# Seven block products instead of eight for one expert pair in four, in the value stage of a PEER layer

## The chip, the cores and the metric

The kernel runs on one core of one Trainium2 chip. The metric is the device time of one execution, in microseconds (us). The kernel before took 2188.84 us (median of three runs: 2188.84, 2189.22 and 2179.97). Engines are named as in the profile: PE multiplies matrices and PEld loads its stationary operand, DVE is the vector engine, ACT the scalar engine, POOL is GpSimd, SP issues the transfers.

## The reference

Two layers, 256 tokens, 1024 channels. Each layer is a mixer (retention, RWKV-7, gated linear attention), an output projection, and a product-key retrieval over 16384 single-neuron experts:

```python
act = gelu(einsum('td,ted->te', xb, u[eidx])) * gate     # 16 experts of each of 8 heads per token
x = x + einsum('te,ted->td', act, v[eidx])
```

The kernel computes it densely. It makes a full matrix of activations, experts by tokens, that is zero where an expert isn't chosen, and multiplies it with all of `v`. This last product, 256 tokens x 16384 experts x 1024 channels, is the value stage.

## The kernel before

One program of 128 expert blocks of 128 experts. `ACTS[:, e, :]` holds the activations of expert block `e`, experts on the partitions and 256 tokens along the row. The values of an expert block are 128 x 1024 numbers, in two halves of 512 channels. Two expert blocks (1 MB) fill one half of `RING`, so `RING` holds one body of four expert blocks, that is eight halves `m = 0..7`.

Every product is in three parts for precision. A number is split into a high part, a cast to fp32r made by ACT (`EH` for the values, `AH` for the activations), and a low part, the rest, made by DVE as a subtraction (`EL`, `AL`). `v_half(m, j)` (L806 to L817) waits for the low parts and, for each of the two token tiles, issues high x high (L814), high x low (L815) and low x high (L816), 512 columns each, added in bank `2 * t + f` of PSUM. So a half is six matmuls, a body 48, and the 32 bodies of a layer 1536.

Nothing plans the order. Each engine has its own instruction queue, in program order, and counting semaphores tie them:

- ACT, `v_split` (L1048) and `a_split` (L1057): the high part of half `m` goes into slot `m % 4` of `EH` once the half four places before has left PE (`v_done`, one count per half). The activations have two slots.
- DVE, `v_lows` (L1688) and `a_lows` (L1692): the low part, once ACT's high part is there (`v_hi`, `a_hi`).
- SP (L366 to L368): reloads a half of the ring once its four low parts are made (`v_lo`).
- After the last body DVE adds the four banks to the residual `X` (L1852), the norm of the next layer begins, and SP clears the semaphores of the layer and releases the next one (`go`).

The first body is written out with the end of the stage before (the `u` stage, which computes the activations), the other 31 are a hardware loop on each engine.

Of the kernel before, what the change touches and what calls it, by code (L numbers as in the profile page):

```python
# [40 lines left out]
P = 128  # L41
# [24 lines left out]
GATE_SCALE = 2.0 ** 15  # L66
D_FEW, P_MANY = (2, 6), (0, 1, 3, 4, 5, 7)
# [35 lines left out]
def trunk(nc, x_in, w_in, w_out, cols, small, rows, norm_final, w_q, keys, u_t, v_t, const, xconst, out):  # L103
    with ExitStack() as ctx:
# [118 lines left out]
        DECODE = PS[:, 0:4, :].rearrange("p b n -> p (b n)").rearrange("p (m u n) -> p m u n", m=8, u=16)  # L223
        FROW = BIG[:, 0:D]
# [54 lines left out]
        vring = [sem("v0_landed"), sem("v1_landed")]  # L279
# [31 lines left out]


# [6 lines left out]
        def _(sp):  # L319
# [10 lines left out]
            with sp.Fori(0, L) as l:  # L330
# [30 lines left out]
                for i in range(2):  # L361
                    sp.wait_ge(*u_lows_made(4 * i + 2, N_BODY - 1, False))
                    sp.wait_ge(*u_lows_made(4 * i + 3, N_BODY - 1, False))
                    sp.dma_start(RING[:, i, :], v_t[l, i]).then_inc(vring[i], 16)
                with sp.Fori(1, 32) as j:
                    for i in range(2):  # L366
                        sp.wait_ge(v_lo, 8 * j + 4 * i - 4)
                        sp.dma_start(RING[:, i, :], v_t[l, 2 * j + i]).then_inc(vring[i], 16)  # L368
                for i in range(2):
                    sp.wait_ge(v_lo, 252 + 4 * i)  # L370
# [15 lines left out]
        def _(pe):  # L386
# [419 lines left out]
            def v_half(m, j, first):  # L806
                e, f = m // 2, m % 2
                pe.wait_ge(v_lo, 8 * j + m + 1)
# [8 lines left out]
                mm.then_inc(v_done, 1)  # L817

            with pe.Fori(0, L) as l:
# [71 lines left out]
                for m in range(8):  # L891
                    v_half(m, 0, True)
                with pe.Fori(1, 32) as j:
                    for m in range(8):
                        v_half(m, j, False)
                pe.wait_ge(v_done, 256)
# [5 lines left out]
        def _(act):  # L902
# [145 lines left out]
            def v_split(m, j, first):  # L1048
                if m % 4 == 0:
                    act.wait_ge(vring[m // 4], 16 * (j + 1))  # L1050
                if first and m < 4:
                    act.wait_ge(u_done, 253 + m)
                else:
                    act.wait_ge(v_done, 8 * j + m - 3)
                act.copy(EH[:, m % 4, :], RING[:, m // 4, (m % 4) * 512:(m % 4 + 1) * 512]).then_inc(v_hi, 1)  # L1055

            def a_split(e, j, first):  # L1057
                if first and e < 2:
                    if e == 0:
                        act.wait_ge(quad_out, 3 + N_QUAD)  # L1060
                else:
                    if first and e == 2:
                        act.wait_ge(u_mul, 2 + 128 - LATE)
                    act.wait_ge(v_done, 8 * j + 2 * e - 2)
                act.copy(AH[:, e % 2, :], ACTS[:, 4 * j + e, :]).then_inc(a_hi, 1)  # L1065

# [5 lines left out]
            with act.Fori(0, L) as l:  # L1072
# [208 lines left out]
        def _(dve):  # L1281
# [480 lines left out]
            with dve.Fori(0, L) as l:  # L1762
# [288 lines left out]
```

## Time and profile before

| what | before |
|---|---|
| median of three runs | 2188.84 us |
| profiled execution, own time | 2180.91 us |
| its span | 2179.1 us |
| PE busy | 2089.8 us, 96% |
| DVE busy | 1441.2 us, 66% |
| ACT busy | 1314.5 us, 60% |
| granted TensorE clock, mean | 0.986 |

The page of the profile gives the busy time of each engine, the span in 40 slices, the chain of work that ended last and the costliest groups of instructions. Busy times of PE overlap, because matmuls are pipelined; the pace is read from the starts. An instruction of DVE or ACT also has a duration longer than the distance to the start of the next one. Shares are averages over stages with different limits: the value stage is the one with 192 GB/s, slices 14 to 20 of the first layer.

### The profile page before, as it was taken

How to read it: one execution, taken by the hardware profiler on the slowest of the kernel's cores; microseconds unless marked ns; L12 is line 12 of the kernel's file. 1: busy time of each engine (PE TensorE's matmuls, PEld its weight loads, DVE VectorE, ACT ScalarE, POOL GpSimd, SP SyncE). 2: the span in 40 equal slices, each digit the busy share in tenths (PEclk: the TensorE clock that was granted, in tenths of full speed). 3: DMA queues.
4: the chain of work that ended last, by engine and by line, in shares of the span. 5: the costliest groups of instructions: out<-in, count | busy, mean ns of one | idle time of the engine just before them, and what ended most of it. 6: DMA issues, size and time to landing. Idle time of an engine off the chain costs nothing.

```text
span 2179.1 us, 45295 instructions
## 1 busy us (share of the span) xinstructions
PE 2089.8 (96%) x14548; PEld 1896.7 (87%) x14548; DVE 1441.2 (66%) x3050; ACT 1314.5 (60%) x3093; POOL 388.9 (18%) x342
## 2 busy tenths in 40 slices
PE   7889899999999999999998998999999999999997
PEld 7889499999999988888788895999999998888886
DVE  5764349778887666666567633496778886666665
ACT  5530145699999655555565302556999995555554
POOL 0312007632222100000003120175322220000000
PEclk9999999999999999999999998999999999999999
DMA  5320244444444555555552102444444445555554
GB/s 210 116 78 1 97 155 165 165 171 157 156 168 157 176 192 192 192 192 192 192 189 97 59 1 98 173 174 166 162 155 170 156 155 191 194 193 192 192 192 184
DMA packets 47464, 338.82 MB, mean 155 GB/s; under 512 B 5649, under 2 KB 5777, under 8 KB 6929
## 3 DMA queue, kind: packets, MB, share of 16 engines
q1 hardware_dynamic: 47376, 337.73, 43.2%
q8 instruction: 46, 0.75, 0.1%
q14 instruction: 42, 0.34, 0.0%
HBM read 336.66 MB, written 1.05 MB: 155 GB/s over the span
## 4 chain that ended last, share of the span: by engine, by line
PE 85%; DVE 9%; ACT 2%; DMA 2%; issue 1%; DVEq 0%; SPq 0%; ACTq 0%; PEldq 0%
PE ps L815 11%; PE ps L814 11%; PE ps L816 11%; PE ps L784 10%; PE ps L786 9%; PE ps L785 9%; PE ps L687 3%; PE ps L407 2%; PE ps L408 2%; PE ps L409 2%; PE ps L550 2%; PE ps L564 1%; PE ps L794 1%; PE ps L795 1%; PE ps L423 1%; DVE expert_lo L1320 1%
## 5 line engine op out<-in xcount | busy, mean ns | idle before, releaser
L784 PE MATMUL ps<-h_t_hi,expert_hi 128*128 128x256 f32 x2048 | 591.3, 289 | 12.3 <-DVE expert_lo L1686 8.5
L785 PE MATMUL ps<-h_t_lo,expert_hi 128*128 128x256 f32 x2048 | 578.5, 282 | 0.0
L786 PE MATMUL ps<-h_t_hi,expert_lo 128*128 128x256 f32 x2048 | 578.2, 282 | 0.0
L1869 POOL TENSOR_TENSOR expert_lo<-w_ring,expert_hi 128x512 fp32r<-128x512 f32 x204 | 289.8, 1429 | 772.1 <-ACT expert_hi L975 770.4
L784 PEld LDWEIGHTS ps<-h_t_hi,expert_hi 128*128 128x128 f32 x2048 | 391.6, 191 | 15.6 <-ACT big L980 8.2
L814 PE MATMUL ps<-expert_hi,act_hi 128*128 128x512 f32 x1024 | 398.4, 389 | 0.0
L815 PE MATMUL ps<-expert_lo,act_hi 128*128 128x512 f32 x1024 | 398.4, 389 | 0.0
L816 PE MATMUL ps<-expert_hi,act_lo 128*128 128x512 f32 x1024 | 398.3, 389 | 0.0
L785 PEld LDWEIGHTS ps<-h_t_lo,expert_hi 128*128 128x128 f32 x2048 | 392.0, 191 | 0.0
L786 PEld LDWEIGHTS ps<-h_t_hi,expert_lo 128*128 128x128 f32 x2048 | 391.6, 191 | 0.0
L975 ACT CAST expert_hi<-w_ring 128x512 fp32r<-128x512 f32 x512 | 308.0, 614 | 98.3 <-PE ps L786 83.7
L1690 DVE TENSOR_TENSOR expert_lo<-w_ring,expert_hi 128x512 fp32r<-128x512 f32 x512 | 331.5, 688 | 6.6 <-ACT expert_hi L1055 6.0
L1065 ACT CAST act_hi<-big 128x256 fp32r (+1 forms) x256 | 104.0, 406 | 321.3 <-PE ps L816 321.3
L1055 ACT CAST expert_hi<-w_ring 128x512 fp32r<-128x512 f32 x512 | 291.8, 617 | 3.2 <-PE ps L786 3.2
L1686 DVE TENSOR_TENSOR expert_lo<-w_ring,expert_hi 128x512 fp32r<-128x512 f32 x308 | 217.6, 718 | 107.1 <-ACT expert_hi L975 104.1
L1694 DVE TENSOR_TENSOR act_lo<-big,act_hi 128x256 fp32r<-128x256 f32 x256 | 108.8, 425 | 256.0 <-ACT act_hi L1065 256.0
L814 PEld LDWEIGHTS ps<-expert_hi,act_hi 128*128 128x128 f32 x1024 | 192.2, 188 | 40.1
L816 PEld LDWEIGHTS ps<-expert_hi,act_lo 128*128 128x128 f32 x1024 | 192.2, 188 | 40.0
L815 PEld LDWEIGHTS ps<-expert_lo,act_hi 128*128 128x128 f32 x1024 | 192.2, 188 | 39.6
L937 ACT CAST expert_hi<-w_ring 128x512 fp32r<-128x512 f32 x168 | 99.8, 621 | 118.9 <-PE ps L425 54.5
L1320 DVE TENSOR_TENSOR expert_lo<-w_ring,expert_hi 128x512 fp32r<-128x512 f32 x168 | 119.4, 749 | 65.4 <-ACT expert_hi L937 63.1
L407 PE MATMUL ps<-h_t_hi,expert_hi 128*128 128x256 f32 x448 | 128.1, 286 | 2.5 <-DVE expert_lo L1320 1.3
(294 smaller groups left out, 3279.2 us busy)
## 6 DMA issues: line engine op xcount, KB each, us to landing
w_ring<-u_t SPq DMA_DIRECT2D x128, 1024.0 KB, 4.8
w_ring<-v_t SPq DMA_DIRECT2D x128, 1024.0 KB, 4.8
w_ring<-w_in SPq DMA_DIRECT2D x32, 1024.0 KB, 4.8
w_ring<-w_q SPq DMA_DIRECT2D x16, 1024.0 KB, 4.8
w_ring<-w_out SPq DMA_DIRECT2D x8, 1024.0 KB, 4.8
big<-xconst SPq DMA_DIRECT2D x2, 1666.0 KB, 9.5
w_ring<-keys SPq DMA_DIRECT2D x2, 1024.0 KB, 4.7
big<-rows SPq DMA_DIRECT2D x2, 576.0 KB, 11.2
```

What stands on the lines that cost most here:

```text
L407: pe.matmul(o, w_hi_m[:, c, :], HTH[:, d, :], start=d == 0, stop=False)
L784: pe.matmul(o, w_hi[:, c, :], HTH[:, d, :], start=d == 0, stop=False)
L785: pe.matmul(o, w_hi[:, c, :], HTL[:, d, :], start=False, stop=False)
L786: mm = pe.matmul(o, w_lo[:, c, :], HTH[:, d, :], start=False, stop=d == DC - 1)
L814: pe.matmul(o, a_hi_t, EH[:, m % 4, :], start=start, stop=False, skip_group_check=True)
L815: pe.matmul(o, a_hi_t, EL[:, m % 4, :], start=False, stop=False, skip_group_check=True)
L816: mm = pe.matmul(o, a_lo_t, EH[:, m % 4, :], start=False, stop=True, skip_group_check=True)
L975: act.copy(EH[:, m % 4, :], RING[:, m // 4, (m % 4) * 512:(m % 4 + 1) * 512]).then_inc(u_hi, 1)
L1055: act.copy(EH[:, m % 4, :], RING[:, m // 4, (m % 4) * 512:(m % 4 + 1) * 512]).then_inc(v_hi, 1)
L1686: dve.tensor_tensor(EL[:, m % 4, :], RING[:, m // 4, (m % 4) * 512:(m % 4 + 1) * 512], EH[:, m % 4, :].bitcast(F32), ALU.subtract).then_in ...
L1690: dve.tensor_tensor(EL[:, m % 4, :], RING[:, m // 4, (m % 4) * 512:(m % 4 + 1) * 512], EH[:, m % 4, :].bitcast(F32), ALU.subtract).then_in ...
L1869: pool.tensor_tensor(EL[:, m % 4, :], RING[:, m // 4, (m % 4) * 512:(m % 4 + 1) * 512], EH[:, m % 4, :].bitcast(F32), ALU.subtract).then_i ...
```

## The change

The 32 bodies of a layer become a first body, 15 turns of two bodies each, and a last body. A turn has eight expert blocks, four pairs. Its first pair is multiplied by the seven-product form of a 2 x 2 block product, where the classic form takes eight block products (two expert blocks by two token tiles by two channel halves). With A the activations (A11, A12: token tile 0, first and second expert block; A21, A22: token tile 1) and B the values (B11, B12: first expert block, two channel halves; B21, B22: second one):

- sums of activations, 128 columns each, in `ASUM`: s1 = A21 + A22, s2 = s1 - A11, s3 = A11 - A21, s4 = A12 - s2
- sums of values, 512 columns each: T1 = B12 - B11, T3 = B22 - B12, T2 = T3 + B11, T4 = B21 - T2
- products, three matmuls each: p1 = A11 B11, p2 = A12 B21, p3 = s4 B22, p4 = A22 T4, p5 = s1 T1, p6 = s2 T2, p7 = s3 T3

p2, p3 and p4 go into the banks of their outputs; p1, p7, p6 and p5 are added up over all turns in the four other banks (4, 7, 6, 5) and folded into `X` and into each other by DVE in and after the last body. The other three pairs are classic (`c`, `d`, `e`, four halves each, six matmuls a half). A turn is 19 units in the order of `V_ORDER`, with the seven products spread between the halves. `V_SLOT` gives each unit one of six slots, two of them new, in memory of the `u` stage. All sums and low parts are made by DVE. The transfers of the values are cut from 1 MB to 512 KB.

The diff, cut to what decides the order of work:

```diff
+V_ORDER = ("p1", "p2", "p3", "c0", "c1", "p7", "c2", "c3", "p6", "d0", "d1", "p5", "d2", "d3", "p4", "e0", "e1", "e2", "e3")
+V_SLOT = (0, 1, 2, 3, 4, 0, 5, 1, 2, 3, 0, 4, 5, 1, 2, 0, 3, 4, 5)
+V_LEN, V_TURNS = len(V_ORDER), N_BODY // 2
+V_ALL = 8 + V_LEN * (V_TURNS - 1) + 8
...
+        VH, VL = ([*(e[:, s, :] for s in range(4)), h[:, 1024:1536], h[:, 1536:2048]] for e, h in ((EH, hth_flat), (EL, htl_flat)))
+        A11H, A2H, ASH = hth_flat[:, 0:128], hth_flat[:, 128:384], hth_flat[:, 512:1024]
+        A11L, A2L, ASL = htl_flat[:, 0:128], htl_flat[:, 128:384], htl_flat[:, 512:1024]
+        T1, T2, T3, T4 = (ht_flat[:, 512 * i:512 * (i + 1)] for i in range(4))
+        ASUM = HOTX[:, 0:512]
+        B11, B12, B21, B22 = (RING[:, 0, 512 * i:512 * (i + 1)] for i in range(4))
...
+        def v_at(name, k):
+            return V_LEN * k - 10 + V_ORDER.index(name)
+        def v_slot(name):
+            return V_SLOT[V_ORDER.index(name)]
+        def slot_left(name, k, first):
+            o = V_ORDER.index(name)
+            s, same = V_SLOT[o], [i for i in range(V_LEN) if V_SLOT[i] == V_SLOT[o]]
+            if o > same[0]:
+                return v_at(V_ORDER[same[same.index(o) - 1]], k)
+            if first:
+                return 5 + s if s < 4 else 1
+            return v_at(V_ORDER[same[-1]], k - 1)
...
+                def load_v(c, j):
+                    half = slice(c % 2 * D, (c % 2 + 1) * D)
+                    sp.dma_start(RING[:, c // 2, half], v_t[l, 2 * j + c // 2, :, half]).then_inc(v_landed[c], 16)
...
-                    sp.dma_start(RING[:, i, :], v_t[l, i]).then_inc(vring[i], 16)
-                with sp.Fori(1, 32) as j:
-                    for i in range(2):
-                        sp.wait_ge(v_lo, 8 * j + 4 * i - 4)
-                        sp.dma_start(RING[:, i, :], v_t[l, 2 * j + i]).then_inc(vring[i], 16)
+                    for c in range(2):
+                        load_v(2 * i + c, 0)
+                for c in range(4):
+                    sp.wait_ge(v_lo, 2 * c + 2)
+                    load_v(c, 1)
+                with sp.Fori(1, V_TURNS) as k:
+                    sp.wait_ge(t_made, 4 * k - 1)
+                    load_v(0, 2 * k)
+                    sp.wait_ge(t_made, 4 * k)
+                    load_v(1, 2 * k)
+                    sp.wait_ge(v_lo, v_at("c1", k))
+                    load_v(2, 2 * k)
+                    sp.wait_ge(v_lo, v_at("c3", k))
+                    load_v(3, 2 * k)
+                    sp.wait_ge(v_lo, v_at("d1", k))
+                    load_v(0, 2 * k + 1)
+                    sp.wait_ge(v_lo, v_at("d3", k))
+                    load_v(1, 2 * k + 1)
+                    sp.wait_ge(v_lo, v_at("e1", k))
+                    load_v(2, 2 * k + 1)
+                    sp.wait_ge(v_lo, v_at("e3", k))
+                    load_v(3, 2 * k + 1)
...
+            def v_product(name, j, bank, a_hi_t, a_lo_t, start):
+                pe.wait_ge(v_lo, v_at(name, j))
+                o, s = PS[:, bank, :], v_slot(name)
+                pe.matmul(o, a_hi_t, VH[s], start=start, stop=False, skip_group_check=True)
+                pe.matmul(o, a_hi_t, VL[s], start=False, stop=False, skip_group_check=True)
+                pe.matmul(o, a_lo_t, VH[s], start=False, stop=True, skip_group_check=True).then_inc(v_done, 1)
+            def v_classic(name, j, e, f):
+                pe.wait_ge(v_lo, v_at(name, j))
+                s = v_slot(name)
+                for t in range(NT):
+                    o = PS[:, 2 * t + f, :]
+                    a_hi_t, a_lo_t = AH[:, e, t * P:(t + 1) * P], AL[:, e, t * P:(t + 1) * P]
+                    pe.matmul(o, a_hi_t, VH[s], start=False, stop=False, skip_group_check=True)
+                    pe.matmul(o, a_hi_t, VL[s], start=False, stop=False, skip_group_check=True)
+                    mm = pe.matmul(o, a_lo_t, VH[s], start=False, stop=True, skip_group_check=True)
+                mm.then_inc(v_done, 1)
...
+                pe.wait_ge(a_lo, 8 * k - 3)
+                v_product("p1", k, 4, A11H, A11L, first)
+                pe.wait_ge(a_lo, 8 * k - 2)
+                v_product("p2", k, 0, A2H[:, a12], A2L[:, a12], False)
+                pe.wait_ge(s_lo, k)
+                v_product("p3", k, 1, ASH[:, s4], ASL[:, s4], False)
+                pe.wait_ge(a_lo, 8 * k - 1)
+                v_classic("c0", k, 0, 0)
+                v_classic("c1", k, 0, 1)
+                v_product("p7", k, 7, ASH[:, s3], ASL[:, s3], first)
+                pe.wait_ge(a_lo, 8 * k)
+                v_classic("c2", k, 1, 0)
+                v_classic("c3", k, 1, 1)
+                v_product("p6", k, 6, ASH[:, s2], ASL[:, s2], first)
+                pe.wait_ge(a_lo, 8 * k + 1)
+                v_classic("d0", k, 0, 0)
+                v_classic("d1", k, 0, 1)
+                v_product("p5", k, 5, ASH[:, s1], ASL[:, s1], first)
+                pe.wait_ge(a_lo, 8 * k + 2)
+                v_classic("d2", k, 1, 0)
+                v_classic("d3", k, 1, 1)
+                v_product("p4", k, 2, A2H[:, a22], A2L[:, a22], False)
+                pe.wait_ge(a_lo, 8 * k + 3)
+                v_classic("e0", k, 0, 0)
+                v_classic("e1", k, 0, 1)
+                pe.wait_ge(a_lo, 8 * k + 4)
+                v_classic("e2", k, 1, 0)
+                v_classic("e3", k, 1, 1)
...
+            def b_high(name, src, j, first):
+                act.wait_ge(v_done, slot_left(name, j, first))
+                act.copy(VH[v_slot(name)], src).then_inc(v_hi, 1)
...
+                left("p1", 1)
+                act.copy(A11H, acts(0, 0, P)).then_inc(a_hi, 1)
+                landed(0, 2 * k - 1)
+                b_high("p1", B11, k, first)
+                landed(1, 2 * k - 1)
+                b_high("p2", B21, k, first)
+                left("p4", 1)
+                act.copy(A2H, acts(1, 0, S)).then_inc(a_hi, 1)
+                act.wait_ge(s_made, 3 * k)
+                left("p5", 1)
+                act.copy(ASH, ASUM).then_inc(s_hi, 1)
+                b_high("p3", B22, k, first)
+                left("e1", 6)
+                act.copy(AH[:, 0, :], acts(2, 0, S)).then_inc(a_hi, 1)
+                landed(2, 2 * k - 1)
+                b_high("c0", ring(4), k, first)
+                b_high("c1", ring(5), k, first)
+                act.wait_ge(t_made, 4 * k - 3)
+                b_high("p7", T3, k, first)
+                left("e3", 8)
+                act.copy(AH[:, 1, :], acts(3, 0, S)).then_inc(a_hi, 1)
+                landed(3, 2 * k - 1)
+                b_high("c2", ring(6), k, first)
+                b_high("c3", ring(7), k, first)
+                act.wait_ge(t_made, 4 * k - 1)
+                b_high("p6", T2, k, first)
+                landed(0, 2 * k)
+                b_high("d0", ring(0), k, first)
+                act.wait_ge(v_done, v_at("c1", k))
+                act.copy(AH[:, 0, :], acts(4, 0, S)).then_inc(a_hi, 1)
+                b_high("d1", ring(1), k, first)
+                b_high("p5", T1, k, first)
+                landed(1, 2 * k)
+                b_high("d2", ring(2), k, first)
+                act.wait_ge(v_done, v_at("c3", k))
+                act.copy(AH[:, 1, :], acts(5, 0, S)).then_inc(a_hi, 1)
+                b_high("d3", ring(3), k, first)
+                act.wait_ge(t_made, 4 * k)
+                b_high("p4", T4, k, first)
+                landed(2, 2 * k)
+                b_high("e0", ring(4), k, first)
+                act.wait_ge(v_done, v_at("d1", k))
+                act.copy(AH[:, 0, :], acts(6, 0, S)).then_inc(a_hi, 1)
+                b_high("e1", ring(5), k, first)
+                landed(3, 2 * k)
+                b_high("e2", ring(6), k, first)
+                act.wait_ge(v_done, v_at("d3", k))
+                act.copy(AH[:, 1, :], acts(7, 0, S)).then_inc(a_hi, 1)
+                b_high("e3", ring(7), k, first)
...
+            def b_low(name, src, j):
+                dve.wait_ge(v_hi, v_at(name, j))
+                dve.tensor_tensor(VL[v_slot(name)], src, VH[v_slot(name)].bitcast(F32), ALU.subtract).then_inc(v_lo, 1)
...
+                s1, s3, s2, s4 = (ASUM[:, i * P:(i + 1) * P] for i in range(4))
+                dve.tensor_tensor(s3, acts(0, 0, P), acts(0, P, S), ALU.subtract)
+                dve.tensor_tensor(s1, acts(0, P, S), acts(1, P, S), ALU.add).then_inc(s_made, 1)
+                a_low(1, A11L, acts(0, 0, P), A11H)
+                dve.wait_ge(s_made, 3 * k - 2)
+                dve.tensor_tensor(s2, s1, acts(0, 0, P), ALU.subtract).then_inc(s_made, 1)
+                b_low("p1", B11, k)
+                dve.wait_ge(s_made, 3 * k - 1)
+                dve.tensor_tensor(s4, acts(1, 0, P), s2, ALU.subtract).then_inc(s_made, 1)
+                b_low("p2", B21, k)
+                dve.tensor_tensor(T3, B22, B12, ALU.subtract).then_inc(t_made, 1)
+                a_low(2, A2L, acts(1, 0, S), A2H)
+                dve.tensor_tensor(T1, B12, B11, ALU.subtract).then_inc(t_made, 1)
+                dve.wait_ge(s_hi, k)
+                dve.tensor_tensor(ASL, ASUM, ASH.bitcast(F32), ALU.subtract).then_inc(s_lo, 1)
+                dve.wait_ge(t_made, 4 * k - 3)
+                dve.tensor_tensor(T2, T3, B11, ALU.add).then_inc(t_made, 1)
+                b_low("p3", B22, k)
+                dve.wait_ge(t_made, 4 * k - 1)
+                dve.tensor_tensor(T4, B21, T2, ALU.subtract).then_inc(t_made, 1)
+                a_low(3, AL[:, 0, :], acts(2, 0, S), AH[:, 0, :])
+                b_low("c0", ring(4), k)
+                b_low("c1", ring(5), k)
+                b_low("p7", T3, k)
+                a_low(4, AL[:, 1, :], acts(3, 0, S), AH[:, 1, :])
+                b_low("c2", ring(6), k)
+                b_low("c3", ring(7), k)
+                b_low("p6", T2, k)
+                b_low("d0", ring(0), k)
+                a_low(5, AL[:, 0, :], acts(4, 0, S), AH[:, 0, :])
+                b_low("d1", ring(1), k)
+                b_low("p5", T1, k)
+                b_low("d2", ring(2), k)
+                a_low(6, AL[:, 1, :], acts(5, 0, S), AH[:, 1, :])
+                b_low("d3", ring(3), k)
+                b_low("p4", T4, k)
+                b_low("e0", ring(4), k)
+                a_low(7, AL[:, 0, :], acts(6, 0, S), AH[:, 0, :])
+                b_low("e1", ring(5), k)
+                b_low("e2", ring(6), k)
+                a_low(8, AL[:, 1, :], acts(7, 0, S), AH[:, 1, :])
+                b_low("e3", ring(7), k)
...
+                    if m == 1:
+                        dve.wait_ge(folded, 1)
+                        plus(T1, PS[:, 6, :])
+                        plus(x11, PS[:, 4, :])
+                    if m == 3:
+                        plus(x22, PS[:, 5, :])
+                    if m == 5:
+                        dve.wait_ge(folded, 2)
+                        plus(x12, T1)
+                dve.tensor_tensor(T2, T1, PS[:, 7, :], ALU.add).then_inc(folded, 1)
+                dve.wait_ge(folded, 5)
+                plus(x12, PS[:, 5, :])
+                dve.wait_ge(folded, 6)
+                plus(x21, T2)
+                plus(x22, T2)
+                dve.wait_ge(folded, 9)
...
```

## Rows read from the trace of the kernel before

**Rows 1.** The page's slices.

```profile
PE   7889899999999999999998998999999999999997
GB/s 210 116 78 1 97 155 165 165 171 157 156 168 157 176 192 192 192 192 192 192 189 97 59 1 98 173 174 166 162 155 170 156 155 191 194 193 192 192 192 184
```

**Rows 2.** The page's chain that ended last, by engine and line.

```profile
PE 85%; DVE 9%; ACT 2%; DMA 2%; issue 1%; DVEq 0%; SPq 0%; ACTq 0%; PEldq 0%
PE ps L815 11%; PE ps L814 11%; PE ps L816 11%; PE ps L784 10%; PE ps L786 9%; PE ps L785 9%; PE ps L687 3%; PE ps L407 2%; PE ps L408 2%; PE ps L409 2%; PE ps L550 2%; PE ps L564 1%; PE ps L794 1%; PE ps L795 1%; PE ps L423 1%; DVE expert_lo L1320 1%
```

**Rows 3.** Busy time by engine in the first layer's value stage.

```profile
core 0: us, PE busy (x) PEld busy (x) DVE busy (x) ACT busy (x) POOL busy (x), PEclk, DMA share, GB/s
737.00:1085.00 348.00, 348.00 (x1537) 287.95 (x1535) 217.66 (x384) 183.64 (x380) 0.00 (x0) 1.00 0.53 189
```

**Rows 4.** Groups of instructions in 850 to 1000 us, value stage.

```profile
L814 PE MATMUL ps<-expert_hi,act_hi 128*128 128x512 f32 x221 | 86.0, 389 | 0.0
L1690 DVE TENSOR_TENSOR expert_lo<-w_ring,expert_hi 128x512 fp32r<-128x512 f32 x112 | 72.4, 688 | 0.0
L1055 ACT CAST expert_hi<-w_ring 128x512 fp32r<-128x512 f32 x111 | 63.2, 617 | 0.0
L1694 DVE TENSOR_TENSOR act_lo<-big,act_hi 128x256 fp32r<-128x256 f32 x55 | 23.4, 425 | 55.8 <-ACT act_hi L1065 55.8
```

**Rows 5.** Timeline of one expert block: start, duration, instruction, [idle before].

```profile
1000.48 0.39 PE L816 MATMUL ps<-expert_hi,act_lo 128*128 128x512 f32 x1
1000.71 0.39 PE L814 MATMUL ps<-expert_hi,act_hi 128*128 128x512 f32 x1
...
1001.00 0.41 ACT L1065 CAST act_hi<-big 128x256 fp32r x1 [1.27 <-PE ps L816]
1001.31 1.14 ACT L1055 CAST expert_hi<-w_ring 128x512 fp32r<-128x512 f32 x2
1001.55 0.42 DVE L1694 TENSOR_TENSOR act_lo<-big,act_hi 128x256 fp32r<-128x256 f32 x1 [1.01 <-ACT act_hi L1065]
1001.96 1.29 DVE L1690 TENSOR_TENSOR expert_lo<-w_ring,expert_hi 128x512 fp32r<-128x512 f32 x2
...
1003.43 0.39 PE L814 MATMUL ps<-expert_hi,act_hi 128*128 128x512 f32 x1
1003.72 0.41 ACT L1065 CAST act_hi<-big 128x256 fp32r x1 [1.27 <-PE ps L816]
```

**Rows 6.** Timeline of DVE, short operations back to back.

```profile
69.24 0.28 DVE L1393 TENSOR_TENSOR big<-big 128x128 f32<-128x128 f32 x1
69.44 0.28 DVE L1392 SCALAR_TENSOR_TENSOR big<-big 128x128 f32<-128x128 f32 x1
...
734.04 0.42 DVE L1694 TENSOR_TENSOR act_lo<-big,act_hi 128x256 fp32r<-128x256 f32 x1
734.37 0.42 DVE L1715 TENSOR_TENSOR big<-big,ps 128x256 f32<-128x256 f32 x1
```

**Rows 7.** Instructions of single lines: duration in ns, min/median/max.

```profile
L1326 DVE TENSOR_TENSOR big<-big x12: 682/686/694, 25.2 to 1140.9; 128x512 f32<-128x512 f32 x12
L1415 DVE TENSOR_SCALAR big<-big x2: 428/428/429, 74.5 to 1154.5; 128x512 f32<-128x512 f32 x2
```

**Rows 8.** Timeline of a stall of PE in the u stage.

```profile
409.72 0.72 DVE L1686 TENSOR_TENSOR expert_lo<-w_ring,expert_hi 128x512 fp32r<-128x512 f32 x1
410.57 0.38 PE L784 MATMUL ps<-h_t_hi,expert_hi 128*128 128x256 f32 x1 [1.57 <-DVE expert_lo L1686]
410.79 0.28 PE L785 MATMUL ps<-h_t_lo,expert_hi 128*128 128x256 f32 x1
410.91 0.28 PE L786 MATMUL ps<-h_t_hi,expert_lo 128*128 128x256 f32 x1
```

**Rows 9.** Transfers: KB each, us to landing (page).

```profile
w_ring<-v_t SPq DMA_DIRECT2D x128, 1024.0 KB, 4.8
x_res<-x_in SPq DMA_DIRECT2D x2, 512.0 KB, 3.8
```

**Rows 10.** Timeline of the end of the first layer.

```profile
1080.84 1.29 DVE L1690 TENSOR_TENSOR expert_lo<-w_ring,expert_hi 128x512 fp32r<-128x512 f32 x2
1083.44 0.39 PE L816 MATMUL ps<-expert_hi,act_lo 128*128 128x512 f32 x1
1083.87 2.64 DVE L1852 TENSOR_TENSOR x_res<-x_res,ps 128x512 f32<-128x512 f32 x4 [1.73 <-PE ps L816]
1084.80 0.39 PE L816 MATMUL ps<-expert_hi,act_lo 128*128 128x512 f32 x1
1088.86 0.11 POOL L1912 MEMSET big<- 128x4 f32 x1 [355.32 <-SPq L376]
1089.94 1.42 DVE L1301 TENSOR_SCALAR big<-x_res,stat 128x1024 f32<-128x1024 f32 x2
```

More of the change, by code:

```diff
@@ new lines, in v_turn @@
+            def v_turn(k, first):
+                a12, a22 = slice(0, P), slice(P, S)
+                s1, s3, s2, s4 = (slice(i * P, (i + 1) * P) for i in range(4))
+                pe.wait_ge(a_lo, 8 * k - 3)
[26 more added lines that the diff above has]
+                v_classic("e3", k, 1, 1)
@@ L891, in _ @@
                 for m in range(8):
[L892 to L896, printed above, removed]
+                    v_half(m, 0, True, 0)
+                v_turn(1, True)
+                with pe.Fori(2, V_TURNS) as k:
+                    v_turn(k, False)
+                for m in range(8):
+                    v_half(m, N_BODY - 1, False, V_ALL - 8)
+                pe.wait_ge(v_done, V_ALL)
                 pe.sem_inc(arrived, 1)
@@ new lines, in a_split @@
+                if first and e == 2:
+                    act.wait_ge(u_mul, 2 + 128 - LATE)
+                if e >= 2:
+                    act.wait_ge(v_done, 2 * e - 2 if first else V_ALL - 10 + 2 * e)
+                elif not first:
+                    act.wait_ge(v_done, v_at(("e1", "e3")[e], V_TURNS - 1))
+                act.copy(AH[:, e % 2, :], ACTS[:, 4 * j + e, :]).then_inc(a_hi, 1)
+            def b_high(name, src, j, first):
+                act.wait_ge(v_done, slot_left(name, j, first))
+                act.copy(VH[v_slot(name)], src).then_inc(v_hi, 1)
@@ new lines, in v_turn, with acts, left, landed @@
+            def v_turn(k, first):
+                def acts(e, t0, t1):
+                    return ACTS[:, bass.ds(8 * k - 4 + e, 1) if not first else slice(4 + e, 5 + e), t0:t1].rearrange("p a n -> p (a n)")
+                def left(name, at_first):
+                    act.wait_ge(v_done, at_first if first else v_at(name, k - 1))
+                def landed(c, j):
+                    act.wait_ge(v_landed[c], 16 * (j + 1))
+                def ring(m):
+                    return RING[:, m // 4, m % 4 * 512:(m % 4 + 1) * 512]
+                left("p1", 1)
[47 more added lines that the diff above has]
+                b_high("e3", ring(7), k, first)
@@ L1696, in hots, with plus @@
+            def plus(x, y):
+                dve.tensor_tensor(x, x, y, ALU.add).then_inc(folded, 1)
+            x11, x12, x21, x22 = (X[:, t, f * 512:(f + 1) * 512] for t in range(NT) for f in range(2))
             def hots(i, q, first):
```

71 lines of the change are left out of this document (43 added, 28 removed).

## The prediction, made before the changed kernel was run

> **What bounds the kernel now.** The slices [rows 1] show the value stage of each layer as a plateau at 192 GB/s with PE at nine tenths or more; slices 14 to 20 are the first layer's. The chain that ended last [rows 2] goes through the three value matmuls with 11% of the span each. The table of that stretch [rows 3] has PE busy for all of its 348 us at full clock (1.00), DVE for 217.66, ACT for 183.64. In the groups [rows 4] the matmuls have 0.0 idle before them, while DVE sits idle only at its activation low part, waiting for ACT, and ACT waits for PE. So PE sets the pace, and the helpers follow it through the slots.
>
> The timeline [rows 5] gives pace and lead. The act_hi cast recurs after 1003.72 - 1001.00 = 2.72 us: one expert block, 12 matmuls, 0.2267 us each. A half is 1.36 us, a body 10.88. The low parts of the next expert block start at 1001.96 and take 1.29 for two. The first is there at 1002.64, and PE takes it at 1003.43: a lead of only 0.79 us, enough as long as nothing is put before it.
>
> **What goes.** 24 matmuls of a pair become 21. A turn had 32 block products of three matmuls, 96 x 0.2267 = 21.76 us; now it has 31, 21.08 us. That is 0.68 us a turn, and 15 turns in two layers give **-20.4 us** if PE is still never kept waiting. It is on the path: nothing else is late in this stage.
>
> **What DVE gets.** Distances between starts are what a queue costs. Two lows of 512 columns take 1.29, one takes 0.68, so the distance is 0.61 [rows 5]. For 256 columns it is 0.33 (734.04 to 734.37), for 128 columns 0.20 (69.24 to 69.44) [rows 6]. A sum of 128x512 out of memory has the same duration as a low part, 0.686 [rows 7], so I take 0.61 for it as well. A turn needs 19 lows, four value sums and the low of ASUM, 24 x 0.61 = 14.6; seven of 256 columns, 2.3; five of 128 columns, 1.0. Together 18.0 us of 21.08. On average it fits. It doesn't fit where it is placed: the turn's first four units last 0.68, 0.68, 0.68 and 1.36 us on PE, and before the fourth DVE has to make nearly all extra work.
>
> **The start of a turn, step by step.** Time 0 is where PE would start p1 without a wait; p2 follows at 0.68, p3 at 1.36, c0 at 2.04. DVE's queue is in order: s3, s1, low of A11, s2, low p1, s4, low p2, T3, low of A2, T1, low of ASUM, T2, low p3, T4, low of the next activations, low c0. Low p1 waits for high p1 on ACT, and that for slot 0, last used by e0 of the turn before.
> - e1, e2 and e3 are 3 x 1.36 = 4.08 us of PE, so e0 ends at -4.08. Its last matmul starts 0.23 before and ends after 0.39: -3.92. ACT starts 0.13 after such an end (1000.48 + 0.39 to 1001.00) [rows 5], DVE 0.04 (1083.44 + 0.39 to 1083.87) [rows 10]; I take 0.09: -3.83.
> - High p1 takes 0.62 [rows 4], DVE starts 0.04 later: -3.17. Was DVE free by then? The cast of the last activations waits for d3 (end -6.12), starts at -5.83, the next cast 0.31 later, low e3 then at -4.87, and s3, s1, A11 and s2 reach low p1 at -3.46. So slot 0 decides, by 0.3 us.
> - From the start of low p1 to the end of low c0: eight steps of 0.61 (p1, p2, T3, T1, ASUM, T2, p3, T4) = 4.88, s4 0.20, two of 0.33 = 0.66, and c0 itself 0.68: 6.42. Low c0 is there at 3.25.
> - PE restarts after a stall 0.13 later (409.72 + 0.72 to 410.57), and its first matmul costs 0.22 where the next costs 0.12, 0.10 more [rows 8]: 3.48.
>
> c0 should start at 2.04, so PE loses **1.44 us a turn**, some 0.4 of it already at p3 (low p3 is there at 1.73 instead of 1.36). Later in the turn DVE isn't late: low d0 comes some 3 us before its use and low e0 2.5, where the slots are given back in PE's own time. ACT has 20 casts of 512 columns in a turn at 1.14 - 0.62 = 0.52 and is ahead all through.
>
> **The first turn** has no slack from the turn before: the first body's last low starts at -3.54 (the lead of the second half, 1.5 us), DVE is free at -2.93, s3, s1, A11 and s2 take it to -2.13. That is 1.04 later than -3.17: 2.48 us. Per layer 14 x 1.44 + 2.48 = 22.6, in two layers **+45.3 us**. Bounds: with the later of all handoffs and 0.04 more for each of 12 steps the turn loses 2.0, with the earlier ones, no slow first matmul and 0.02 less a step 1.0; that is +32 to +62.
>
> **The fold.** Four adds stand in the last body, at 0.61, where DVE idles 1.01 of each 2.72 us [rows 4, 5]; the slots keep the delay inside the leads. After the last low, which starts at 1081.45 and gives DVE back at 1082.06 in the kernel before, stand four adds (T2, and three into X): 2.44, and the wait for the last one's end 0.1, so 1084.6 where the final adds started at 1083.87 [rows 10]. They are DVE-bound, so **+0.7 a layer, +1.4**. If the adds in the last body delay PE as well, at most their 2.44 a layer. More semaphores to clear: go comes at about 1088.8 (POOL's memset), the norm at 1089.94 is what PE needs [rows 10], so a microsecond hides them.
>
> **Transfers.** Eight issues a turn instead of four. 512 KB land in 3.8 us, 1 MB in 4.8 [rows 9]. The tightest is the first quarter of the second body: freed by T2 at about 1.1, landed by 5.0, and d0's cast is due at about 5 with its low due in DVE's queue at 6.5. Hidden, with 0.9 us to spare; beyond that a late landing would be paid in every turn.
>
> **The sum.** -20.4 + 45.3 + 1.4 = +26.3 us. The profiled execution took 2180.91, so 2207.2. The median of the runs shown lies 7.9 above it, two of three at 2189, and the changed kernel should fall the same way: 2188.84 + 26.3 = **2215 us**.
>
> **A rule beside it.** The two lows in 1.29 us [rows 5] show that a DVE operation starts 0.07 before the one in front has ended. The Trainium skill, "VectorE: DVE Perf Modes", section "The DRAIN you can't avoid", says that the next operation doesn't start until the pipe is empty, and adds that one that is not held starts earlier. By its first sentence each step costs its whole duration, the second rival below; by the row and its second sentence the sum stands.
>
> **The rivals.**
> - *PE never waits, 2170 us.* If DVE keeps its average lead, as 18.0 of 21.08 us and six slots suggest, only -20.4 + 1.4 = -19.0 stays. It decides at the start of the turn: break-even is at (20.4 - 1.4) / 30 = 0.63 us of delay a turn, so my walk of 7.4 us from e0's end to c0 would have to be 0.8 too long. Against it: eight steps of 0.61 alone are 4.9 us behind slot 0's release, of 6.12 there are.
> - *Whole durations in the chain, 2242 us.* If sums and lows of different tiles don't overlap: eight of 0.688, 0.28, two of 0.425 and 0.69 are 7.32 instead of 6.42, 0.90 more in 30 turns, +27. The waits of DVE for its own sums speak for it a little, but an operation stands between each sum and its reader; the row of 1.29 speaks against.
> - *The plain sums run in a faster form, 2184 us, no change.* A 128x512 operation with one input tile takes 0.428, 0.26 less [rows 7]. Four sums so would save 1.04 in each walk, leave 0.40 of 1.44, and bring the sum to about -5. Against it: the sum with two input tiles took 0.686 in the same rows.
>
> **How the numbers follow.** Forecast 0.60, with 2202 to 2232 as its own range (the stalls' bounds); PE never waits 0.15; whole durations or another longer walk 0.13; fast sums or a walk near break-even 0.12. The measurement tells about 0.5%, 11 us, from no change. Faster 0.16, same 0.13, slower 0.71. The range leaves out most of the first rival and the far end of the second: 2186 to 2244.
>
> **What would show it.** Right: PE has two idle spells a turn ended by DVE, about 0.4 us before p3 and 1 us before c0, none before d0, e0 or p5; the turn takes 22.5 us; DVE runs without idle from low p1 to low c0; high p1 starts just after e0's last matmul. Wrong: turns of 21.1 us without idle on PE; idle at other units; sums shorter than 0.68; or PE waiting for a cast or a transfer, which would mean that ACT or SP, not DVE, holds the turn.

## The result: 1.2% slower, and the profile after

| | before | changed |
|---|---|---|
| median | 2187.16 us (4 runs) | 2213.27 us (4 runs, 2203.60 to 2219.61) |
| ratio, 95% interval | | 1.0123 [1.0098, 1.0148] |
| profiled execution, span | 2179.1 us | 2210.6 us |
| DVE / PE busy | 1441.2 / 2089.8 us | 1596.6 / 2095.7 us |
| value stage, layer 1 | 736.84 to 1085.19: 348.35 us | 742.82 to 1101.65: 358.83 us |
| one turn (two bodies) | 21.76 us | 22.39 us |

The forecast was 2215 us, range 2186 to 2244.

The page of the changed kernel, chain that ended last and two of the costliest groups, which answer to [rows 2, 4]:

```profile
PE 76%; DVE 16%; issue 3%; ACT 3%; DMA 2%; DVEq 1%; SPq 0%; ACTq 0%; PEldq 0%
...
L1886 DVE TENSOR_TENSOR expert_lo<-w_ring,expert_hi 128x512 fp32r<-128x512 f32 x300 | 206.4, 688 | 62.3 <-ACT expert_hi L1179 58.4
L885 PE MATMUL ps<-expert_hi,act_hi 128*128 128x512 f32 x420 | 166.9, 397 | 17.3 <-DVE expert_lo L1886 17.3
```

The waits of PE, by line waited for (us in total, times, longest):

```profile
PE ps L885 <- DVE expert_lo L1886: 17.3, 30, 0.6
...
PE ps L874 <- DVE expert_lo L1886: 6.7, 30, 1.2
```

DVE's share of the chain went from 9% to 16%. L885 is the first matmul of a classic half, L874 that of one of the seven products, and each waits 30 times: once in each of the 15 turns of two layers. Where in the turn, PE's timeline tells; only rows with idle time before them were kept:

```profile
913.16 0.50 PE L874 MATMUL ps<-expert_hi,h_t_hi 128*128 128x512 f32 x1 [0.15 <-DVE expert_lo L1886]
...
914.71 0.50 PE L885 MATMUL ps<-expert_hi,act_hi 128*128 128x512 f32 x1 [0.58 <-DVE expert_lo L1886]
...
935.55 0.50 PE L874 MATMUL ps<-expert_hi,h_t_hi 128*128 128x512 f32 x1 [0.15 <-DVE expert_lo L1886]
...
937.09 0.50 PE L885 MATMUL ps<-expert_hi,act_hi 128*128 128x512 f32 x1 [0.58 <-DVE expert_lo L1886]
```

Two waits, 1.55 us apart, every 935.55 - 913.16 = 22.39 us, and none elsewhere: p3 and c0. Idle is counted from the modelled end of the matmul before (0.39 us after its start), so it shows 0.16 less than the starts are apart beyond their usual distance. The loss is 22.39 - 21.08 = 1.31 us a turn; the two waits, 0.16 added to each, and 0.10 more for the slow matmul behind each make 1.25 of it.

What stands in front of c0 is in DVE's and ACT's timeline of the same turn:

```profile
907.18 0.39 PE L887 MATMUL ps<-expert_hi,act_lo 128*128 128x512 f32 x1
...
907.61 0.62 ACT L1179 CAST expert_hi<-w_ring 128x512 fp32r<-128x512 f32 x1 [0.82 <-PE ps L887]
...
907.84 0.29 DVE L1906 TENSOR_TENSOR hot_extra<-hot_extra,big 128x128 f32<-128x128 f32 x1
...
908.26 0.69 DVE L1886 TENSOR_TENSOR expert_lo<-w_ring,expert_hi 128x512 fp32r<-128x512 f32 x1
908.87 0.28 DVE L1909 TENSOR_TENSOR hot_extra<-big,hot_extra 128x128 f32<-128x128 f32 x1
909.08 0.68 DVE L1886 TENSOR_TENSOR expert_lo<-w_ring,expert_hi 128x512 fp32r<-128x512 f32 x1
909.68 0.68 DVE L1911 TENSOR_TENSOR h_t<-w_ring 128x512 f32<-128x512 f32 x1
910.28 0.42 DVE L1896 TENSOR_TENSOR h_t_lo<-big,h_t_hi 128x256 fp32r<-128x256 f32 x1
910.62 0.68 DVE L1913 TENSOR_TENSOR h_t<-w_ring 128x512 f32<-128x512 f32 x1
911.22 0.68 DVE L1915 TENSOR_TENSOR h_t_lo<-hot_extra,h_t_hi 128x512 fp32r<-128x512 f32 x1
911.82 0.68 DVE L1917 TENSOR_TENSOR h_t<-h_t,w_ring 128x512 f32<-128x512 f32 x1
912.42 0.68 DVE L1886 TENSOR_TENSOR expert_lo<-w_ring,expert_hi 128x512 fp32r<-128x512 f32 x1
913.03 0.68 DVE L1920 TENSOR_TENSOR h_t<-w_ring,h_t 128x512 f32<-128x512 f32 x1
913.63 0.42 DVE L1896 TENSOR_TENSOR act_lo<-big,act_hi 128x256 fp32r<-128x256 f32 x1
913.97 0.68 DVE L1886 TENSOR_TENSOR expert_lo<-w_ring,expert_hi 128x512 fp32r<-128x512 f32 x1
```

e0's last matmul ends at 907.57, and 0.04 later ACT casts p1. The low of p1 follows at 908.26, and from there DVE works without a gap, the 512-column operations 0.60 us from start to start, through the four value sums (L1911 T3, L1913 T1, L1917 T2, L1920 T4) to the low of c0, which ends at 914.65. PE begins c0 at 914.71.

**Where the 31.5 us between the spans are.** Value stages: 358.83 - 348.35 = 10.48 in the first layer and as much in the second, 21.0. End of the layers: the final adds end 1.77 us after PE's last matmul where it was 1.32, 0.9 together. End of the program: 0.4, which is DVE's wait for the transfer of `norm_final`, first in the kernel before, then in the changed one:

```profile
2173.43 2.48 DVE L1860 SCALAR_TENSOR_TENSOR big<-x_res,stat,big 128x1024 f32<-128x1024 f32 x2 [0.73 <-DMA big<-norm_final]
2204.92 2.48 DVE L2132 SCALAR_TENSOR_TENSOR big<-x_res,stat,big 128x1024 f32<-128x1024 f32 x2 [1.17 <-DMA big<-norm_final]
```

SP issues it behind the clearing of the semaphores, and the changed kernel has seven more of them, some 0.06 us each. That is the change: **+22.3 us**. The rest lies in stages whose code is the same. The 6.0 ahead of the first value stage go with the granted clock there (last section). Of the 3.2 between the layers, 0.67 stand right before PE's first matmul of the second layer, which starts 1.56 us after the norm's last instruction on DVE has ended, where it was 0.89; what ends this wait wasn't traced. The other 2.5 come with a lower clock again: 0.66 in the 20 us behind the value stage, where it was 0.83.

### The profile page after: what moved, and what is told of

It is laid out like the page before. It is cut to its first block, busy times and chain, and to the rows that moved or that the text cites. A ratio compares the mean times of both kernels' runs of the same rounds, so it can differ in the third digit from the quotient of the medians.

```text
span 2210.6 us, 46003 instructions
## 1 busy us (share of the span) xinstructions
PE 2095.7 (95%) x14458; PEld 1881.7 (85%) x14458; DVE 1596.6 (72%) x3426; ACT 1380.4 (62%) x3215; POOL 389.3 (18%) x342
## 4 chain that ended last, share of the span: by engine, by line
PE 76%; DVE 16%; issue 3%; ACT 3%; DMA 2%; DVEq 1%; SPq 0%; ACTq 0%; PEldq 0%
PE ps L835 10%; PE ps L837 9%; PE ps L836 9%; PE ps L885 6%; PE ps L887 6%; PE ps L886 6%; PE ps L738 3%; DVE expert_lo L1886 2%; PE ps L458 2%; PE ps L460 2%; PE ps L459 2%; PE ps L601 2%; PE ps L615 1%; PE ps L474 1%; PE ps L845 1%
## 5 line engine op out<-in xcount | busy, mean ns | idle before, releaser
L836 PE MATMUL ps<-h_t_lo,expert_hi 128*128 128x256 f32 x2048 | 578.5, 282 | 0.0
L837 PE MATMUL ps<-h_t_hi,expert_lo 128*128 128x256 f32 x2048 | 578.3, 282 | 0.0
L1081 ACT CAST expert_hi<-w_ring 128x512 fp32r<-128x512 f32 x512 | 308.2, 614 | 98.4 <-PE ps L837 83.9
L1873 DVE TENSOR_TENSOR expert_lo<-w_ring,expert_hi 128x512 fp32r<-128x512 f32 x308 | 217.8, 719 | 107.1 <-ACT expert_hi L1081 104.2
L1179 ACT CAST expert_hi<-w_ring 128x512 fp32r<-128x512 f32 x300 | 182.9, 619 | 144.4 <-PE ps L887 80.5
L1886 DVE TENSOR_TENSOR expert_lo<-w_ring,expert_hi 128x512 fp32r<-128x512 f32 x300 | 206.4, 688 | 62.3 <-ACT expert_hi L1179 58.4
L885 PE MATMUL ps<-expert_hi,act_hi 128*128 128x512 f32 x420 | 166.9, 397 | 17.3 <-DVE expert_lo L1886 17.3
L1043 ACT CAST expert_hi<-w_ring 128x512 fp32r<-128x512 f32 x168 | 99.8, 621 | 119.5 <-PE ps L476 54.9
L1507 DVE TENSOR_TENSOR expert_lo<-w_ring,expert_hi 128x512 fp32r<-128x512 f32 x168 | 119.4, 749 | 65.1 <-ACT expert_hi L1043 62.8
L886 PE MATMUL ps<-expert_lo,act_hi 128*128 128x512 f32 x420 | 163.6, 390 | 0.0
L887 PE MATMUL ps<-expert_hi,act_lo 128*128 128x512 f32 x420 | 163.5, 389 | 0.0
L459 PE MATMUL ps<-h_t_lo,expert_hi 128*128 128x256 f32 x448 | 126.7, 283 | 0.0
L460 PE MATMUL ps<-h_t_hi,expert_lo 128*128 128x256 f32 x448 | 126.7, 283 | 0.0
L885 PEld LDWEIGHTS ps<-expert_hi,act_hi 128*128 128x128 f32 x420 | 78.8, 188 | 45.7 <-DVE expert_lo L1886 28.3
L885 PE MATMUL ps<-h_t_hi,act_hi 128*128 128x512 f32 x300 | 116.8, 389 | 0.0
L887 PE MATMUL ps<-h_t_hi,act_lo 128*128 128x512 f32 x300 | 116.7, 389 | 0.0
```

The costliest lines, as they stand in the source:

```text
L836: pe.matmul(o, w_hi[:, c, :], HTL[:, d, :], start=False, stop=False)
L837: mm = pe.matmul(o, w_lo[:, c, :], HTH[:, d, :], start=False, stop=d == DC - 1)
L885: pe.matmul(o, a_hi_t, VH[s], start=False, stop=False, skip_group_check=True)
L886: pe.matmul(o, a_hi_t, VL[s], start=False, stop=False, skip_group_check=True)
L887: mm = pe.matmul(o, a_lo_t, VH[s], start=False, stop=True, skip_group_check=True)
L1179: act.copy(VH[v_slot(name)], src).then_inc(v_hi, 1)
```

## The experiments

Each is an edit of the changed kernel, but for the one that is an edit of the kernel before. The kernel before ran beside them: 2187.32 us beside the first four, 2187.54 beside the other three. The two theories are the same in all: PE waits for what stands in DVE's in-order queue at the start of a turn; or the work as such (contention, transfers, slots) costs, wherever it stands.

**One sum behind c0.**

```diff
                 b_low("p3", B22, k)
-                dve.wait_ge(t_made, 4 * k - 1)
-                dve.tensor_tensor(T4, B21, T2, ALU.subtract).then_inc(t_made, 1)
                 a_low(3, AL[:, 0, :], acts(2, 0, S), AH[:, 0, :])
                 b_low("c0", ring(4), k)
+                dve.wait_ge(t_made, 4 * k - 1)
+                dve.tensor_tensor(T4, B21, T2, ALU.subtract).then_inc(t_made, 1)
```

> The changed kernel with one value sum (T4) moved in DVE's queue from before the low of c0 to behind it; the same work. Theory (PE waits for DVE's in-order queue between slot 0's release and the low of c0): the path is one step of 0.605 us shorter, so the turn falls from 22.39 to 21.78 us, PE's wait before c0 vanishes or nearly so while the short one before p3 stays, and the time falls by 30 x 0.61 = 18 us, from 2213 to 2195. Rival (the turn is long because PE, ACT, DVE and the smaller transfers contend, or because a transfer or slot comes late): the same work at another place leaves 22.39 us a turn and 2213 us.

Measured: 2191.93 us (10 runs, 2187.71 to 2202.76), 1.0030 [1.0009, 1.0051] of before. PE's waits in the same stretch:

```profile
912.18 0.50 PE L874 MATMUL ps<-expert_hi,h_t_hi 128*128 128x512 f32 x1 [0.15 <-DVE expert_lo L1886]
...
933.98 0.50 PE L874 MATMUL ps<-expert_hi,h_t_hi 128*128 128x512 f32 x1 [0.15 <-DVE expert_lo L1886]
```

The turn is 933.98 - 912.18 = 21.80 us, 0.59 less. The wait before c0 is gone and that before p3 is as it was, since T4 stands behind p3. The first value stage takes 349.9 us, 8.9 less than in the changed kernel, so the two stages give back 17.9 of the 21 us between the medians. The same work one place later gives back one step: the rival fails here.

**All four sums behind the lows.**

```diff
-                dve.tensor_tensor(T3, B22, B12, ALU.subtract).then_inc(t_made, 1)
                 a_low(2, A2L, acts(1, 0, S), A2H)
-                dve.tensor_tensor(T1, B12, B11, ALU.subtract).then_inc(t_made, 1)
...
                 b_low("c0", ring(4), k)
+                dve.tensor_tensor(T3, B22, B12, ALU.subtract).then_inc(t_made, 1)
+                dve.tensor_tensor(T1, B12, B11, ALU.subtract).then_inc(t_made, 1)
+                dve.wait_ge(t_made, 4 * k - 3)
+                dve.tensor_tensor(T2, T3, B11, ALU.add).then_inc(t_made, 1)
...
                 b_low("c2", ring(6), k)
+                dve.wait_ge(t_made, 4 * k - 1)
+                dve.tensor_tensor(T4, B21, T2, ALU.subtract).then_inc(t_made, 1)
```

> The changed kernel with all four value sums moved behind the low of c0 (T3, T1, T2 just behind it, T4 behind the low of c2); the same work. Theory: from the start of low p1 to the end of low c0 four steps less, 6.40 - 2.42 = 3.98 us, so c0's low is there at 0.8 us of the turn where PE needs it at 2.04, and the turn is 21.08 us, PE never idle. From 2213: 30 x 1.31 = 39 and a further 2 for the first turns, 2172 us, faster than before's 2187. What could be late next is c1 (low 0.15 us before its use). Rival (contention): 22.39 us and 2213. Rival (the walk is only shifted): the waits turn up at c1, p7 or d0, with 21.7 us or more a turn.

Measured: 2166.70 us (5 runs, 2164.69 to 2168.36), 0.9910 [0.9890, 0.9930] of before: faster than both. The stretches of 150 us in this kernel (the columns as in [rows 3]) and, for comparison, in the changed one:

```profile
850.00:1000.00 150.00, 150.00 (x663) 124.10 (x662) 130.38 (x260) 95.91 (x200) 0.00 (x0) 1.00 0.59 199
```

```profile
850.00:1000.00 150.00, 145.65 (x629) 116.78 (x628) 122.84 (x241) 91.99 (x189) 0.00 (x0) 1.00 0.58 190
```

PE is busy all through, with DVE at 87%. Its first products of two turns:

```profile
938.81 0.39 PE L874 MATMUL ps<-expert_hi,h_t_hi 128*128 128x512 f32 x1
...
959.91 0.39 PE L874 MATMUL ps<-expert_hi,h_t_hi 128*128 128x512 f32 x1
```

A turn is 21.10 us. The low of c0 is there 3.97 us after the start of low p1 (expected 3.98). So the mere order decides between 26 us lost and 21 us won in the medians. The value stage takes 339.3 us in each layer, 9.0 less than before and 19.5 less than in the changed kernel: 39.0 us are the order's. The median, 47 us lower and 5 below what was expected, holds some 8 us more, which lie outside the value stages. One wait is left in each layer, at c1 of the first turn:

```profile
752.20 0.50 PE L885 MATMUL ps<-h_t_hi,act_hi 128*128 128x512 f32 x1 [0.60 <-DVE h_t_lo L1886]
```

So the second rival, that the waits only move, holds for the first turn, where the wait before c0 is now one before c1, and fails for the other fourteen.

**The sums cut to eight columns.** In all turns but the first; order and all else unchanged. The kernel leaves out 504 of the 512 columns of each value sum, so its result is not the layer's; it serves for the time alone.

```diff
+                w = 512 if first else 8
-                dve.tensor_tensor(T3, B22, B12, ALU.subtract).then_inc(t_made, 1)
+                dve.tensor_tensor(T3[:, 0:w], B22[:, 0:w], B12[:, 0:w], ALU.subtract).then_inc(t_made, 1)
...
```

> The changed kernel where T1 to T4 are computed over 8 of 512 columns in all turns but the first, so part of the value product is left out; order, casts, lows, matmuls and transfers as they are. Theory: four steps of 0.605 fall to about 0.1 each, some 2.0 us a turn, more than the 1.31 that PE loses, so 21.08 us a turn and about 2174 us. Together with the kernel that moves the sums it tells whether their mere place costs, or their amount. Rival (contention of casts, lows and transfers, or late slots): the turn stays above 22 us, since only 4 of 24 long DVE operations shrink.

Measured: 2174.11 us (4 runs), 0.9936 [0.9911, 0.9962]. The value stage of the first layer takes 340.5 us, 1.2 more than with the sums moved. The first turn, which keeps its full sums, waits as in the changed kernel (1.20 and 0.60 there), and no turn after it does:

```profile
750.51 0.47 PE L874 MATMUL ps<-expert_hi,h_t_hi 128*128 128x512 f32 x1 [1.20 <-DVE expert_lo L1886]
752.06 0.47 PE L885 MATMUL ps<-expert_hi,act_hi 128*128 128x512 f32 x1 [0.62 <-DVE expert_lo L1886]
```

So the loss is the sums' time in the path, and no share of it is left for the other 20 long operations, the casts or the transfers.

**One more operation of 128x512 in front of T3.**

```diff
+                dve.tensor_tensor(HOTX[:, 512:1024], B22, B12, ALU.subtract)
                 dve.tensor_tensor(T3, B22, B12, ALU.subtract).then_inc(t_made, 1)
```

> The changed kernel with one more 128x512 subtraction on DVE (into memory that nothing reads) in front of T3. Theory: one step more on the path, 22.39 + 0.605 = 23.0 us a turn, PE's waits before p3 and c0 grow by 0.61 in sum, time 2213 + 18 = 2231 us. Rival (DVE has 3 us of slack a turn, so the average decides): no change, 2213.

Measured: 2225.90 us (4 runs), 1.0180 [1.0155, 1.0204]. The waits:

```profile
917.77 0.50 PE L874 MATMUL ps<-expert_hi,h_t_hi 128*128 128x512 f32 x1 [0.75 <-DVE expert_lo L1886]
...
919.31 0.50 PE L885 MATMUL ps<-expert_hi,act_hi 128*128 128x512 f32 x1 [0.58 <-DVE expert_lo L1886]
...
940.76 0.50 PE L874 MATMUL ps<-expert_hi,h_t_hi 128*128 128x512 f32 x1 [0.75 <-DVE expert_lo L1886]
```

22.99 us a turn, 0.60 more, all of it at p3, whose wait grew from 0.15 to 0.75. DVE is idle for 4 us of a turn (27.16 of the 150 us in the row of the changed kernel), and none of it serves the start of the turn. With the two kernels that move sums, the dose is one step per operation: 22.99, 22.39, 21.80, and 21.10 where PE is the bound. The median came out 5 us lower than expected; the turn didn't.

**p1 in an earlier slot.**

```diff
-V_SLOT = (0, 1, 2, 3, 4, 0, 5, 1, 2, 3, 0, 4, 5, 1, 2, 0, 3, 4, 5)
+V_SLOT = (1, 0, 2, 3, 4, 0, 5, 1, 2, 3, 0, 4, 5, 1, 2, 0, 3, 4, 5)
```

> The changed kernel with p1 and p2 exchanging their first slots: p1 takes slot 1, given back by d3 two microseconds earlier than slot 0 by e0. Theory: slot 0's release is what the start of low p1 hangs on, but only by some 0.2 us (s2 starts at 907.84 in the trace of the changed kernel, so DVE could have begun low p1 at 908.04 instead of 908.26); then DVE's own queue behind e3 decides. 22.39 falls to about 22.17 us a turn, 2213 to 2207. If the slot alone were the cause of the wait, 1.31 us a turn would go: 21.1 and 2174. If it has no part, 22.39 and 2213.

Measured: 2206.20 us (4 runs), 1.0095 [1.0071, 1.0118]. The wait that is left:

```profile
913.00 0.50 PE L885 MATMUL ps<-expert_hi,act_hi 128*128 128x512 f32 x1 [0.58 <-DVE expert_lo L1886]
...
935.17 0.50 PE L885 MATMUL ps<-expert_hi,act_hi 128*128 128x512 f32 x1 [0.58 <-DVE expert_lo L1886]
```

22.17 us a turn, 0.22 less. Slot 0 is what the path begins with, but a slot given back 2 us earlier brings only 0.22, because DVE's queue stands right behind it: the low of p1 now starts at 906.58, 0.21 after s2 and without idle, as the short operations before it follow each other.

**The kernel before with small loads.**

```diff
-                        sp.dma_start(RING[:, i, :], v_t[l, 2 * j + i]).then_inc(vring[i], 16)
+                        for h in range(2):
+                            sp.dma_start(RING[:, i, h * D:(h + 1) * D], v_t[l, 2 * j + i, :, h * D:(h + 1) * D]).then_inc(vring[i], 16)
...
-                    act.wait_ge(vring[m // 4], 16 * (j + 1))
+                    act.wait_ge(vring[m // 4], 32 * (j + 1))
```

> The kernel before, with its value loads cut into two transfers of 512 KB each, as in the change, and nothing else. Theory: the transfers are hidden, the expert block stays at 2.72 us, the stage at 348.3 us and the time at 2187. Rival (twice the packets and issues slow the casts or lows, or come late): more than 2.72 us a block; if it were to carry the loss seen, 20 to 40 us more.

Measured: 2187.51 us (10 runs), 1.0005 [0.9988, 1.0022]. ACT's casts show the pace:

```profile
1002.24 0.41 ACT L1067 CAST act_hi<-big 128x256 fp32r x1 [1.27 <-PE ps L818]
...
1004.96 0.41 ACT L1067 CAST act_hi<-big 128x256 fp32r x1 [1.26 <-PE ps L818]
```

2.72 us a block, as in [rows 5], and 348.35 us for the stage, with 65,895 packets instead of 47,464. The cut of the transfers by itself costs nothing that the stage or the interval shows.

**The sums moved, and the fold moved too.** The sums are moved as above; of the edit only the fold is shown.

```diff
...
                     if m == 3:
                         plus(x22, PS[:, 5, :])
+                        plus(x12, PS[:, 5, :])
                     if m == 5:
-                        dve.wait_ge(folded, 2)
+                        dve.wait_ge(folded, 5)
                         plus(x12, T1)
-                dve.tensor_tensor(T2, T1, PS[:, 7, :], ALU.add).then_inc(folded, 1)
-                dve.wait_ge(folded, 5)
-                plus(x12, PS[:, 5, :])
-                dve.wait_ge(folded, 6)
+                        dve.tensor_tensor(T2, T1, PS[:, 7, :], ALU.add).then_inc(folded, 1)
+                dve.wait_ge(folded, 7)
```

> The kernel with the four value sums moved behind the lows, and in addition two of the four adds that stood behind the last low (T2, and bank 5 into x12) moved into the last body, into DVE's idle spells. Theory: the final adds are no longer late: they start right behind the last but one half, 0.6 us earlier, and the end of the layer is 0.4 us earlier, 0.8 in all, which the median can hardly tell: 2166 us. In the trace the first final add starts 0.04 us after PE's last but one half has ended, as in the kernel before.

Measured: 2171.60 us (6 runs, 2164.39 to 2175.75), 0.9934 [0.9914, 0.9955]. DVE's last adds, and the last matmuls of PE's last two halves:

```profile
1079.23 1.28 DVE L1946 TENSOR_TENSOR x_res<-x_res,h_t 128x512 f32<-128x512 f32 x2
1081.16 2.57 DVE L2123 TENSOR_TENSOR x_res<-x_res,ps 128x512 f32<-128x512 f32 x4 [0.65 <-PE ps L867]
```

```profile
1080.67 0.39 PE L867 MATMUL ps<-expert_hi,act_lo 128*128 128x512 f32 x1
...
1082.03 0.39 PE L867 MATMUL ps<-expert_hi,act_lo 128*128 128x512 f32 x1
```

The last but one half ends at 1081.06 and the final adds begin 0.10 later (0.04 was expected). They end 1083.73 - 1082.42 = 1.31 us after PE, as in the kernel before, where the kernel with only the sums moved has 1.77: 0.46 us a layer given back, as meant. The median lies 5 us above the other's all the same. The profiled executions differ ahead of the value stage, which starts at 743.1 against 737.1 us, with the same code in front, while the stage itself takes 339.3 us in both. So which of the two is the faster by its median was not settled; that both beat the kernel before was.

## Why the prediction was right, step by step

- *What goes, -20.4.* Right. Turns of 21.10 us with PE never idle are 0.66 below 21.76, where 0.68 was worked out.
- *The walk from low p1 to low c0, 6.42 us.* Right: 914.65 - 908.26 = 6.39. The plain sums take 0.68 and start 0.60 apart, as the lows do, so the third rival (sums in a faster form) fell at once; and an overlap of 0.08 between different operations holds throughout, so the second (whole durations) fell too. The Trainium skill, "VectorE: DVE Perf Modes", section "The DRAIN you can't avoid", says that the next operation doesn't start until the pipe is empty, and that one that is not held starts earlier. The first sentence, read as a step of the whole duration, as the prediction weighed it, isn't borne out here; the second is: the next one starts 0.60 us after one that takes 0.68.
- *The delay, 1.44 us a turn: 1.31.* The terms that were a little large are the handoffs. ACT began 0.04 after e0's last matmul (0.09 was taken) and PE 0.06 after the low of c0 (0.13, from the one stall in [rows 8]); with 0.03 of the walk that is 0.15. The slow first matmul was 915.04 - 914.71 = 0.33 where others follow after 0.227: 0.10, as taken.
- *The first turn, 2.48.* Right, with 0.15 too much: from its p1 to the next turn's p1 it takes 777.16 - 753.73 = 23.43 us, 2.33 more than the 21.10 of a turn without waits.
- *Slot 0 decides by 0.3 us.* Right in kind; the slot exchange gave 0.22.
- *The fold, +1.4.* Measured +0.9. The final adds took 2.48 where they took 2.64 when one of them waited for PE.
- *More semaphores to clear, nothing.* This term was not nothing. POOL's memset, its first instruction behind `go`, comes 2.76 us after the end of the final adds instead of 2.35. At the end of the program the 0.4 us are paid: DVE waits for `norm_final` for 0.99 to 1.37 us in the changed kernel and its variants, 0.73 and 0.69 in the kernel before and the one with small loads. Between the layers PE's first matmul comes 1.06 to 1.56 us after the norm in the former and 0.89 and 0.99 in the latter; that the clearing is the cause there too wasn't shown.
- *Transfers hidden.* Right, with less margin than worked out: 512 KB land in 4.5 us by the page, not in the 3.8 taken, and ACT sits idle 1.99 us for one of them before it casts d0; DVE still comes to d0 without idle. The kernel with small loads and the one with the sums moved, where PE waits for none, settle it.
- *The sum.* +26.3 forecast; the change itself is +22.3 in the profiled pair. The waits were put 4.0 too high (2 x (14 x 1.31 + 2.33) = 41.3 instead of 45.3), the fold 0.5 too high, the clearing 0.4 too low. That the medians differ by 26.1, as forecast to 0.2, is luck: they hold some 4 us more than the change. By the mean granted clock of whole runs: the one run of the changed kernel with 0.984 took 2203.60 us, and those of the kernel before with 0.984 took 2179.81 to 2181.98, 22 to 24 apart. The 1.7 us between 2215 and 2213.27 are the kernel before's own median, 2188.84 then and 2187.16 with one run more.
- The first rival, that PE never waits, was wrong for this order of DVE's queue and right for another: it named 2170 us, and with the sums moved the kernel takes 2166.70.

## What to carry to other kernels

An engine with a fifth of its time free can still be the bound, if its queue is in order and its extra work stands in front of what is needed next: walk from the release of the first slot to the first late operand, one start distance per instruction, and compare that with what the consumer does meanwhile. Where work has to be added to such a queue, put what is used late (here the value sums, used 5 to 15 us into the turn) behind what is used at once; four moved operations made 39 us in the two value stages, 47 in the medians.

## What the runs showed of the hardware beyond that

The granted clock of one stretch differs from trace to trace with the same code in it: the last steps of the mixer with the output projection, ahead of the first value stage. First the kernel before, then the changed one, 215 to 230 and 230 to 245 us (columns as in [rows 3]):

```profile
215.00:230.00 15.00, 15.00 (x107) 11.71 (x106) 2.07 (x6) 0.00 (x0) 0.00 (x0) 1.00 0.00 1
230.00:245.00 15.00, 14.85 (x40) 7.72 (x39) 8.08 (x15) 0.21 (x1) 0.00 (x0) 0.77 0.12 39
```

```profile
215.00:230.00 15.00, 15.00 (x77) 10.83 (x77) 2.07 (x6) 0.00 (x0) 0.00 (x0) 0.71 0.01 1
230.00:245.00 15.00, 15.00 (x42) 10.42 (x42) 5.04 (x11) 0.21 (x1) 0.00 (x0) 0.50 0.00 0
```

The granted clock falls from 2.4 to 1.2 GHz out of a stretch in which PE is busy for 15.00 of 15 us, and PE stays busy (14.85 and 15.00) while it is low: by these shares for (1 - 0.77) x 15 / 0.5 = 7 us in the one trace, and for (1 - 0.71) x 15 / 0.5 + 15 = 24 us in the other. The value stage then starts at 736.84 or at 742.82 us. In the seven experiments it starts at 735.4 to 737.1 us three times and at 742.4 to 746.0 four times; the kernel before with small loads is among the first, the one with the fold moved among the second. The clock of these two stretches tells them apart: 1.00, then 0.77 to 0.89, in the four traces that start early, and 0.69 to 0.81, then 0.50 or 0.51, in the five that start late. What decides it was not found, and it is 6 us that no edit here touched, more than the fold is worth.
